# Giving each partition eight neighbouring rows of the experts' gate and up weights

## What is computed

```python
def moe(xn, w_router, w_gate, w_up, w_down):
    logits = (xn @ w_router).astype(jnp.float32)
    top_val, top_idx = lax.top_k(logits, TOP_K)
    top_w = jax.nn.softmax(top_val, axis=-1)
    ...
        hg = jnp.einsum('sd,edf->sef', xs, w_gate)
        hu = jnp.einsum('sd,edf->sef', xs, w_up)
        hh = jax.nn.silu(hg) * hu * gs[..., None].astype(xs.dtype)
        return jnp.einsum('sef,efd->sd', hh, w_down)
```

## Time and profile before

| | us |
|---|---|
| median of 3 runs | 1267.6 |
| lowest and highest | 1265.0, 1268.31 |
| the profiled execution, its own time | 1265.41 |
| span of its profile, first to last instruction | 1263.6 |
| TensorE matmuls busy in the span | 1206.0 (95%) |
| TensorE weight loads busy | 615.0 (49%) |
| VectorE, ScalarE busy | 320.0, 248.7 |
| moved by DMA | 413.66 MB, mean 327 GB/s |

### The profile page before, as it was taken

The page is one execution under the profiler, slowest core; times in us unless marked ns, Lnnn a source line. Parts: engine busy times, 40 slices in busy tenths (PEclk is TensorE's granted clock), DMA queues, the critical chain, the costliest instruction groups (busy, mean ns, idle before and its releaser), DMA issues.

```text
span 1263.6 us, 20291 instructions
## 1 busy us (share of the span) xinstructions
PE 1206.0 (95%) x8367; PEld 615.0 (49%) x8368; DVE 320.0 (25%) x722; ACT 248.7 (20%) x438; POOL 27.9 (2%) x44
## 2 busy tenths in 40 slices
PE   6989999999899999897999999999999999999997
PEld 4755777788665634332333433433343343334333
DVE  2363666667454510100010010010001101000102
ACT  2251433333154111010010201102100210211111
POOL 2100000000010100000000000000000000000000
PEclk9999999999999799999999999999999999999999
DMA  9611745326713599999999999999999999999994
GB/s 337 223 67 56 271 142 198 127 107 218 284 64 119 196 416 426 419 420 427 421 419 423 421 419 422 425 419 419 425 419 417 424 423 419 422 424 405 414 427 173
DMA packets 73165, 413.66 MB, mean 327 GB/s; under 512 B 6606, under 2 KB 11852, under 8 KB 64636
## 3 DMA queue, kind: packets, MB, share of 16 engines
q1 hardware_dynamic: 71708, 409.60, 80.0%
q0 software_dynamic: 1088, 1.81, 0.4%
q10 hardware_dynamic: 288, 1.05, 0.2%
HBM read 411.39 MB, written 1.05 MB: 326 GB/s over the span
## 4 chain that ended last, share of the span: by engine, by line
PE 78%; DMA 11%; DVE 4%; issue 2%; ACT 2%; SPq 2%; POOL 0%; DVEq 0%; ACTq 0%; POOLq 0%
PE ps L1437 16%; PE ps L1417 11%; DMA ring<-in_moe_w_up 7%; PE ps L1412 6%; PE ps L1395 6%; DMA ring<-in_moe_w_down 4%; PE ps L1121 4%; PE ps L1117 4%; PE ps L1118 4%; PE ps L1399 3%; PE ps L1504 3%; PE ps L1468 3%; PE ps L1290 2%; PE ps L1102 2%; PE ps L1488 2%
## 5 line engine op out<-in xcount | busy, mean ns | idle before, releaser
L1437 PE MATMUL ps<-ring,arena 128*64 128x448 f32 x640 | 249.8, 542 | 10.3 <-DMA ring<-in_moe_w_up 4.2
L1438 PE MATMUL ps<-ring,arena 128*64 128x448 f32 x640 | 250.0, 543 | 0.0
L1417 PE MATMUL ps<-ring,arena 128*32 128x448 f32 x1152 | 161.4, 539 | 0.0
L1437 PEld LDWEIGHTS ps<-ring,arena 128*64 128x64 f32 x640 | 84.0, 137 | 156.7 <-issue 142.8
L1418 PE MATMUL ps<-ring,arena 128*32 128x448 f32 x384 | 160.0, 539 | 0.0
L1981 DVE TENSOR_TENSOR arena<-arena,ps 64x448 f32<-64x448 f32 (+1 forms) x64 | 38.5, 613 | 372.6 <-ACT arena L902 193.8
L1504 PE MATMUL ps<-ring,arena 128*64 128x512 f32 x280 | 125.1, 596 | 4.2 <-DMA ring<-in_moe_w_down 4.2
L1505 PE MATMUL ps<-ring,arena 128*64 128x512 f32 x280 | 125.1, 596 | 0.0
L1412 PE MATMUL ps<-ring,arena 128*32 128x448 f32 x768 | 90.4, 542 | 6.4 <-DVE arena L1981 4.0
L1417 PEld LDWEIGHTS ps<-ring,arena 128*32 128x32 f32 x1152 | 48.0, 110 | 93.8 <-issue 93.8
L1721 DVE TENSOR_TENSOR w_lo<-ring,w_hi 128x2048 fp32r<-128x2048 f32 x33 | 75.5, 2292 | 60.4 <-ACT w_hi L794 58.9
(11 more groups left out here) (292 smaller groups left out, 1423.1 us busy)
## 6 DMA issues: line engine op xcount, KB each, us to landing
ring<-in_moe_w_down SPq DMA_DIRECT2D x64, 1792.0 KB, 21.0
ring<-in_moe_w_gate SPq DMA_DIRECT2D x127, 896.0 KB, 21.2
ring<-in_moe_w_up SPq DMA_DIRECT2D x127, 896.0 KB, 21.9
ring<-in_ffn_w_gate SPq DMA_DIRECT2D x5, 2048.0 KB, 7.8
ring<-in_ffn_w_up SPq DMA_DIRECT2D x5, 2048.0 KB, 7.9
ring<-in_ffn_w_down SPq DMA_DIRECT2D x5, 2048.0 KB, 7.7
ring<-in_mla_w_o SPq DMA_DIRECT2D x2, 2048.0 KB, 24.2
ring<-in_swa_w_q SPq DMA_DIRECT2D x2, 2048.0 KB, 8.5
```

Of the source, the lines that this page charges most:

```text
L1417: pe.matmul(ps[32 * j:32 * j + 32, c, 0:CH], thirds[j], wu[:, c * CH:(c + 1) * CH], start=first, stop=last)
L1437: pe.matmul(ps[0:NARROW, c, 0:CH], lhs, wu[:, cols], start=(k == 0), stop=(k == KD - 1))
L1438: mm = pe.matmul(ps[64:64 + NARROW, c, 0:CH], lhs, wg[:, cols], start=(k == 0), stop=(k == KD - 1))
```

## The change

The views of the gate and up weights give partition p the eight neighbouring rows 8p to 8p + 7, so piece k holds row 8p + k on partition p. The gather must give the features in the same order, so for block k it takes every eighth column of `xn`, from column k on. The order in which the products are summed over features is the only thing that differs in the result. Shapes, sizes and order of the DMAs, the ring and all waits are the same.

```diff
-        eg = e_gate[0].rearrange("e (k p) f -> p e k f", p=P)
-        eu = e_up[0].rearrange("e (k p) f -> p e k f", p=P)
+        eg = e_gate[0].rearrange("e (p k) f -> p e k f", p=P)
+        eu = e_up[0].rearrange("e (p k) f -> p e k f", p=P)
         ed = e_down[0].rearrange("e (a p j) n -> p e a (j n)", a=2, p=P)
...
                 for k in range(KD):
                     for t in range(TT):
-                        mm = pe.matmul(ps[...], xn[:, t, k * P:(k + 1) * P], sel[:, t, :],
+                        mm = pe.matmul(ps[...], xn[:, t, :].rearrange("s (p k) -> s k p", k=KD)[:, k, :], sel[:, t, :],
                                        start=(t == 0), stop=(t == TT - 1))
```

More of the change, by code:

```diff
@@ L1385, in gather @@
                     for t in range(TT):
-                        mm = pe.matmul(ps[:, GATHER_BANK + k // 4, (k % 4) * SLOTS:(k % 4 + 1) * SLOTS], xn[:, t, k * P:(k + 1) * P], sel[:, t, :],
+                        mm = pe.matmul(ps[:, GATHER_BANK + k // 4, (k % 4) * SLOTS:(k % 4 + 1) * SLOTS], xn[:, t, :].rearrange("s (p k) -> s k p", k=KD)[:, k, :], sel[:, t, :],
                                        start=(t == 0), stop=(t == TT - 1))
```

## The result

The changed kernel takes 1305.91 us (4 runs, 1302.08 to 1309.07) against 1266.43 for the kernel before: a ratio of 1.031, interval 1.029 to 1.033. It is 39.5 us slower, where 0.2 us was predicted. The profiled execution took 1309.07 us with a span of 1307.1; it is the slowest of the four, so its trace shows some 3 us more of loss than the median.

A forecast was written before the change was run, and what follows sets the result against it. The DMA engines were taken as the bound, with TensorE only filling their queue. First gather +0.2 us, seven middle and last gathers hidden, DMAs 0: +0.2 us, giving a median of 1267.8 us, range 1263 to 1274.5.

The forecast's parts named there:

- the term of 0: Gate and up DMAs: rows 114,688 B apart instead of 14,336 B cost nothing, bounds -7.4 to +7.6 us.
- The choice by the down pieces' distance: Down pieces already jump 57,344 B between partitions at 421 and 424 GB/s, so twice that distance was taken as free.
- Rivals two and three: Gate and up DMAs: rows far apart read slower (+7.6 us, chance 0.08) or faster (-7.4 us, chance 0.12).
- The pace of the strided load: Gather's weight loads: a strided fp32 load goes at 0.12 us at full clock against 0.113, +0.2 us a gather.
- The first rival: Gather: strided loads slow as in the transposes, +4.8 us at x1.5 or +12.1 us at x2.2; chance 0.13.
- x2.2: Gather loads in the first rival: the transposes' 130 against 58 ns, strided against contiguous, with the fixed part taken off.
- The room of 6.1 us: Behind a gather in a wide item: TensorE may run 10.8 - 4.7 = 6.1 us later before the DMA engines idle.
- seven middle gathers: Gathers between first and last: growth of +0.2 us each, or +4.4 at most in the rival, hidden under the DMA queue.
- a trap: Chain of waits: its 78% for PE against 11% for DMA was said to mislead, ignoring how long DMAs stood queued.
- Each us on this gather moves the whole stream: First gather: the next DMA issues only after products step 1, so the gather's growth counts in full, forecast +0.2 us.
- The 3.7 us of TensorE's work ahead of the first gather: Before the first gather, at granted clock 0.50: TensorE busy 3.7 of 6.4 us, with waits between the router's small steps.
- the 0.5 that I had found there: Last gather, ahead of the last DMA's landing: its growth is free up to 0.5 us and counts beyond.

The follow-up runs named there:

- e1_rows_only: The changed kernel with the old contiguous gather, keeping only the new gate and up weight rows (products of other pairs): 1266.96 us, ratio 1.0001.
- e11_half: The kernel before with only the first row tile in each gather, 16 loads: 1267.9 us, ratio 1.0009.
- e9_fewer_bytes: The kernel before, each gate and up piece loading 1536 of its 1792 columns from the second expert on: 1256.53 us, ratio 0.991.
- e10_wide_moving: The changed kernel with each gather matmul's moving operand given twice, 192 columns in place of 96: 1293.58 us, ratio 1.021.
- e8_bench: The kernel before plus, after its last scatter, groups of eight matmuls and eight transposes reading the ring at various steps; its total time means nothing.

## Why the prediction was wrong

**DMAs: right in the price.** The rows' new distance costs nothing, as the term of 0 had it. The choice by the down pieces' distance held, at twice that distance (e1_rows_only: 421 GB/s, ratio 1.0001). Rivals two and three are out. The stream did get longer, from the 805.7 us of the earlier trace rows to some 833 (first new DMA at 445.36, last landing near 1278.8), but because TensorE asked for its pieces later.

**The pace of the strided load: the first step that failed.** The prediction took 0.12 us "nearly today's pace of the gather" from the transposes of line 1488; it is 0.238. The pace of one kind of instruction was carried over to another. A transpose's load goes at step 2 from 141 ns to some 206 and stays there, and its pace stays near 0.12 us; the load of an fp32 matmul goes from 192 to 334 ns at step 8, and its pace from 0.113 to 0.238. The first rival had the right mechanism, at a chance of 0.13. That its x2.2 is so near to the measured 0.238 / 0.113 = x2.1 is luck: the factor came from the same transposes, whose own pace the stride hardly changes.

**The room of 6.1 us: the second step that failed, and in the rival too.** Even at x2.2 the rival came only to +12.1 us, since its seven middle gathers "still fit under 6.1 us". That was a stock, used up once, and I spent it at every gather. What fills it up again is the difference between the two engines' times over two items, 210.5 - 209.7 = 0.8 us. In the changed kernel the DMA engines run dry behind the fourth, sixth and eighth gather only (behind the fifth and the seventh the share stays at 1.00 for 833.5 to 839.5 and 1055.4 to 1061.4 us), and yet each gather costs its 6.0 us: TensorE has become the bound, and the holes in the stream only follow from it. Two numbers of the kernel before could have told. PE idles 805.70 - 784.74 = 21.0 us in the whole stream, which is less than the 7 x 4.4 = 30.8 that the rival hid there. And of these its waits for the ring's DMAs, between 440 and 1247.2 us, are 10.8 us:

```profile
PE ps L1437 <- DMA ring<-in_moe_w_up: 4.2, 4, 1.1
PE ps L1504 <- DMA ring<-in_moe_w_down: 4.2, 5, 1.4
...
PE ps L1412 <- DMA ring<-in_moe_w_up: 2.4, 3, 0.8
```

The chain of waits with PE at 78%, which I called a trap, was a fair warning: in the steady part both engines were within 0.4% of being the bound.

**The clock: not in the sum at all.** The prediction saw the low clock only in the first gather. In the changed kernel it falls in each of the eight later gathers (0.50 to 0.52 for the 6 us from some 5 us into it) and, in the one shown, stays low for 4.1 us of the down steps behind it, 2.0 us each. The 3.7 us of TensorE's work ahead of the first gather, as the prediction has them, are 4.07 (PE busy from 419 to 425.43 us); nothing hangs on it.

**The first gather: nearly harmless.** Its loads take 7.71 us where they took 6.75, +1.0, where the rival had 3.4 to 8.2: the strided loads follow each other every 0.238 us at either clock level, while contiguous ones take 0.207 at the low clock and 0.113 at the full one. "Each us on this gather moves the whole stream" was too simple, as e11_half shows for a shorter gather.

**The account.** Here are the first and last gathers of the changed kernel and of e9_fewer_bytes (where line 1386 has become 1387).

```profile
428.52 7.71 PEld L1386 LDWEIGHTS ps<-arena,xn 128*128 128x128 f32 x32
...
1272.10 7.71 PEld L1386 LDWEIGHTS ps<-arena,xn 128*128 128x128 f32 x32
```

```profile
425.94 6.90 PEld L1387 LDWEIGHTS ps<-arena,xn 128*128 128x128 f32 x32
...
1225.18 3.69 PEld L1387 LDWEIGHTS ps<-arena,xn 128*128 128x128 f32 x32
```

TensorE's way from the first gather to the last is 1225.2 - 425.9 = 799.3 us in e9_fewer_bytes, in the kernel before it is 1234.2 - 425.4 = 808.8 and in the changed one 1272.1 - 428.5 = 843.6. So the change adds 44.3 us to TensorE (eight gathers including the first, of which seven with 4.0 + 2.0 us are 42), 9.5 of them hidden under the DMAs: +34.8. (Of these 9.5 us, 7.9 lie between the second gather and the fourth, where the kernel before takes 217.6 us and e9_fewer_bytes 209.8: there TensorE still waits for DMAs, behind the idle stretch at the start.) Behind the start of the last gather the changed kernel takes 1307.1 - 1272.1 = 35.0 and the one before 1263.6 - 1234.2 = 29.4: +5.6, the last gather's 4.0 and 2.0 less the 0.5 that I had found there. The first gather starts 3.1 us later (428.5 against 425.4), ahead of anything changed, and 2.7 of them are there by 153 us into the span (line 1172 begins at 155.7 against 153.0). Each kernel has only one trace here, and they don't sort by stride: 424.9 with strided loads in e10_wide_moving, 428.4 with contiguous ones in e8_bench. Why is open. The sum is 34.8 + 5.6 + 3.1 = 43.5, the difference of the two spans. It is 4 us more than the 39.5 of the medians: the traced execution of the changed kernel lies 3.2 us above its median, that of the kernel before 1.0 below.

## What to carry to other kernels

Where two resources are both near full, compare their times over one period of the loop before calling any growth hidden: a queue's depth pays once, only the difference of the periods pays every time. In these runs the stationary operand of an fp32 matmul loaded at full pace only with its values at most two apart; if an order of columns has to change, change it where the data is written, once, not in loads that repeat. Measure a stride with the very form of instruction that will use it, since here the loads of a transpose and of a matmul reacted at different steps, and only the matmul's pace fell.

## What was not expected of the hardware

- Load time of an fp32 matmul's stationary operand, 128 columns: 192, 196, 260, 327 ns at steps 1 to 4, and 308 to 338 at 5 to 17, with the pace of the loads the same at granted clocks 0.5 and 1.0 (0.238 us).
- Transposes: 141 ns at step 1, 206 at step 2, 207 at step 4, with the pace of the loads at 0.11 and 0.12 us.
- TensorE's clock fell to 1.2 GHz while the engine was busy without a gap, with a 96-column matmul every 0.238 us; with 192 columns at the same pace it did not.
- A VectorE scalar_tensor_tensor of 1024 columns with both fp32 inputs at a step of 8 takes 2.09 to 2.12 us, contiguous 1.285.
- Gather blocks of four strided loads put between down steps cost 1.26 us each, 10.1 for eight; in one piece eight such blocks cost 7.7.
